# A two-layer decoder trunk in f32r: the moving operand of the large matmuls is walked in four sweeps, and the ring slots are shifted by 64 bytes

## The reference

```python
for i in range(2):                      # DEPTH
    if i == 0:
        h = h + stick_breaking_mixer(rmsnorm(h, sb_norm), w_qkv, w_o)    # 16 heads of 128
    else:
        h = h + chunked_gmlp_mixer(rmsnorm(h, gm_norm), w_in, v_norm, w_s, b_s, w_o)
    g, u = split(rmsnorm(h, ffn_norm[i]) @ w_gate_up[i], 2)              # 2048 x 11264
    h = h + (silu(g) * u) @ w_down[i]                                     # 5632 x 2048
return rmsnorm(h, final_norm)
```

## Time and profile before

| | |
|---|---|
| median of 2 runs | 2096.86 us (2096.85 to 2096.87) |
| the profiled execution | 2096.69 us |
| its span, first to last instruction | 2095.0 us |
| PE busy | 2085.6 us |
| DVE busy | 1430.4 us |
| ACT busy | 1012.8 us |
| DMA | 402.47 MB, mean 192 GB/s |
| granted TensorE clock, mean | 0.999 |

### The profile page before, as it was taken

The page is one execution under the profiler, slowest core; times in us unless marked ns, Lnnn a source line. Parts: engine busy times, 40 slices in busy tenths (PEclk is TensorE's granted clock), DMA queues, the critical chain, the costliest instruction groups (busy, mean ns, idle before and its releaser), DMA issues.

```text
span 2095.0 us, 27155 instructions
## 1 busy us (share of the span) xinstructions
PE 2085.6 (100%) x9279; PEld 1727.3 (82%) x9279; DVE 1430.4 (68%) x1822; ACT 1012.8 (48%) x1285; POOL 16.4 (1%) x30
## 2 busy tenths in 40 slices
PE   9999999999999999999999999999999999999998
PEld 7888888888888888888888888888888888888887
DVE  6787777867666666665557887877666676664444
ACT  6677765544444444444445444554444444444443
POOL 1000000000000000000000000000000000000000
PEclk9999999999999999999999999999999999999999
DMA  8564655666666666555567665566666666655554
GB/s 272 181 186 155 190 180 171 202 194 194 192 191 196 193 192 192 196 194 192 192 198 207 186 204 187 188 186 202 195 187 196 193 195 192 191 194 197 191 191 150
DMA packets 207419, 402.47 MB, mean 192 GB/s; under 512 B 12336, under 2 KB 13056, under 8 KB 206976
## 3 DMA queue, kind: packets, MB, share of 16 engines
q1 hardware_dynamic: 206496, 398.11, 60.9%
q0 software_dynamic: 688, 3.18, 0.4%
q10 hardware_dynamic: 176, 0.40, 0.1%
HBM read 399.55 MB, written 2.10 MB: 192 GB/s over the span
## 4 chain that ended last, share of the span: by engine, by line
PE 99%; issue 0%; ACT 0%; DVE 0%; POOLq 0%; POOL 0%; DVEq 0%; ACTq 0%
PE acc L1091 65%; PE acc L1097 32%; PE tp L1173 1%; PE tp L1193 0%; PE tp L1322 0%; PE acc L1139 0%; PE tp L1105 0%; PE acc L1132 0%; PE acc L1365 0%; PE acc L1364 0%; PE acc L1363 0%; ACT xT L372 0%; PE tp L1181 0%; PE tp L1125 0%; DVE h L1060 0%
## 5 line engine op out<-in xcount | busy, mean ns | idle before, releaser
L662 DVE TENSOR_TENSOR w_lo<-raw,w_hi 128x1024 fp32r<-128x1024 f32 x750 | 915.8, 1224 | 583.5 <-ACT w_hi L354 579.7
L354 ACT ACTIVATE w_hi<-raw 128x1024 fp32r<-128x1024 f32 x750 | 792.9, 1060 | 920.3 <-PE acc L1097 915.0
L1091 PE MATMUL acc<-w_hi,xT 128*128 128x512 f32 x4080 | 1010.3, 390 | 0.0
L1091 PEld LDWEIGHTS acc<-w_hi,xT 128*128 128x128 f32 x4080 | 764.7, 188 | 157.9
L1097 PE MATMUL acc<-w_lo,xT 128*128 128x512 f32 x2040 | 545.3, 389 | 0.0
L1097 PEld LDWEIGHTS acc<-w_lo,xT 128*128 128x128 f32 x2040 | 383.0, 188 | 79.6
L1091 PE MATMUL acc<-w_hi,hid_hi 128*128 128x512 f32 x944 | 368.4, 390 | 0.0
L1091 PE MATMUL acc<-w_hi,hid_lo 128*128 128x512 f32 x944 | 367.3, 389 | 0.0
L1097 PE MATMUL acc<-w_lo,hid_hi 128*128 128x512 f32 x944 | 252.3, 389 | 0.0
L1097 PEld LDWEIGHTS acc<-w_lo,hid_hi 128*128 128x128 f32 x944 | 177.2, 188 | 36.8
L1091 PEld LDWEIGHTS acc<-w_hi,hid_lo 128*128 128x128 f32 x944 | 177.3, 188 | 36.7
(11 more groups left out here) (117 smaller groups left out, 429.4 us busy)
## 6 DMA issues: line engine op xcount, KB each, us to landing
raw<-in_ffn_w_gate_up SPq DMA_DIRECT2D x352, 512.0 KB, 4.5
raw<-in_ffn_w_down SPq DMA_DIRECT2D x176, 512.0 KB, 3.6
raw<-in_sb_w_qkv SPq DMA_DIRECT2D x95, 512.0 KB, 4.4
raw<-in_gm_w_in SPq DMA_DIRECT2D x64, 512.0 KB, 4.2
raw<-in_sb_w_o SPq DMA_DIRECT2D x32, 512.0 KB, 4.1
raw<-in_gm_w_o SPq DMA_DIRECT2D x32, 512.0 KB, 3.9
h<-in_x SPq DMA_DIRECT2D x3, 512.0 KB, 8.9
gain_bc<-in_gm_v_norm POOLq DMA_DIRECT2D x1, 1024.0 KB, 6.8
```

Of the source, the lines that this page charges most:

```text
L354: nc.scalar.activation(w_hi[:, p % RING], raw[:, p % RING], ACT.Copy).then_inc(hi_ready, 1)
L662: nc.vector.tensor_tensor(w_lo[:, p % RING], raw[:, p % RING], w_hi[:, p % RING].bitcast(f32), ALU.subtract).then_inc(lo_ready, 1)
L1091: nc.tensor.matmul(acc_at(chunk, r), part[:, kt, rs], w_hi[:, p % RING, k], start=(kt == 0 and part is hi), stop=False)
```

## The change

The matmuls with weights as moving operand are told to take its 512 columns, and to write the 512 columns of acc, in another order. `swept` turns a row of 512 columns into a pattern of 4 sweeps x 32 runs x 4 columns: the first sweep takes columns 0-3, 16-19, 32-35 and so on, the second 4-7, 20-23 and so on. Four f32 columns are 16 bytes, and the runs of a sweep are 64 bytes apart. Operand and output are rearranged alike, so each column still goes to its own place. The stationary operand, the number of instructions, all waits and the tensors' contents are as before. The row is 128 x 512 in every case.

`ring` allocates w_hi and w_lo with 16 more columns per slot, so that a slot stands 4160 bytes behind the one before it: slots 0 to 3 at 0, 64, 128 and 192 bytes off a multiple of 256. A whole ring is then 16640 bytes, again a multiple of 256. W0 is the address at which w_hi began, and `region` is kept at a multiple of 512 bytes from it.

```diff
+    LINE, SWEEPS = 4, 4
...
-        w_hi = sb("w_hi", [P, RING, KP, CH], f32r)
-        w_lo = sb("w_lo", [P, RING, KP, CH], f32r)
+        STEP = 16
+
+        def ring(name):
+
+            return sb(name, [P, RING, KP * CH + STEP], f32r)[:, :, 0:KP * CH].rearrange("p s (k n) -> p s k n", k=KP)
+
+        w_hi = ring("w_hi")
+        w_lo = ring("w_lo")
+        W0 = nc.lookup_mloc(raw).addr + RING * KP * CH * 4
...
-        lead_in = sb("lead_in", [P, (nc.lookup_mloc(w_hi).addr - used_up_to) % CH // 4])
+        lead_in = sb("lead_in", [P, (W0 - used_up_to) % CH // 4])
...
+        def swept(columns):
+
+            return columns.rearrange("p (c h e) -> p h c e", h=SWEEPS, e=LINE)
...
-                            nc.tensor.matmul(acc_at(chunk, r), part[:, kt, rs], w_hi[:, p % RING, k],
+                            nc.tensor.matmul(swept(acc_at(chunk, r)), part[:, kt, rs], swept(w_hi[:, p % RING, k]),
                                              start=(kt == 0 and part is hi), stop=False)
...
-                        last = nc.tensor.matmul(acc_at(chunk, r), hi[:, kt, r * P:(r + 1) * P],
-                                                w_lo[:, p % RING, k], start=False, stop=(kt == K - 1))
+                        last = nc.tensor.matmul(swept(acc_at(chunk, r)), hi[:, kt, r * P:(r + 1) * P],
+                                                swept(w_lo[:, p % RING, k]), start=False, stop=(kt == K - 1))
```

More of the change, by code:

```diff
@@ L106, in hybrid_trunk @@
         used_up_to = nc.lookup_mloc(moments).addr + 32
-        lead_in = sb("lead_in", [P, (nc.lookup_mloc(w_hi).addr - used_up_to) % CH // 4])
+        lead_in = sb("lead_in", [P, (W0 - used_up_to) % CH // 4])
         region = sb("region", [P, 2 * KF * S])
         R0 = nc.lookup_mloc(region).addr
-        assert (R0 - nc.lookup_mloc(w_hi).addr) % CH == 0
+        assert (R0 - W0) % CH == 0
         HB = KF * S * 4
@@ L1138, in early_products @@
                 for r in range(RT):
-                    last = nc.tensor.matmul(acc_at(0, r), part[:, kt, r * P:(r + 1) * P], weight[:, p, k],
+                    last = nc.tensor.matmul(swept(acc_at(0, r)), part[:, kt, r * P:(r + 1) * P], swept(weight[:, p, k]),
                                             start=(kt == 0 and part is xT_hi and weight is w_hi), stop=False)
@@ L1356, in _ @@
                 rs = slice(r * P, (r + 1) * P)
-                dst = acc_at(1, r)
+                dst = swept(acc_at(1, r))
                 for t in range(ROWWISE, 2 * PF):
@@ L1362, in _ @@
                         kt = (t - PF) * KP + k
-                        nc.tensor.matmul(dst, hid_hi[:, kt, rs], w_hi[:, t % RING, k], start=False, stop=False)
-                        nc.tensor.matmul(dst, hid_hi[:, kt, rs], w_lo[:, t % RING, k], start=False, stop=False)
-                        last = nc.tensor.matmul(dst, hid_lo[:, kt, rs], w_hi[:, t % RING, k], start=False,
+                        nc.tensor.matmul(dst, hid_hi[:, kt, rs], swept(w_hi[:, t % RING, k]), start=False, stop=False)
+                        nc.tensor.matmul(dst, hid_hi[:, kt, rs], swept(w_lo[:, t % RING, k]), start=False, stop=False)
+                        last = nc.tensor.matmul(dst, hid_lo[:, kt, rs], swept(w_hi[:, t % RING, k]), start=False,
                                                 stop=(kt == KF - 1))
```

## The result

The changed kernel took 2113.4 us (median of 2 runs, 2113.0 to 2113.8) against 2096.9 us: slower by 0.8%, ratio 1.0079 with a 95% interval of 1.0062 to 1.0095. The forecast was 2010 us and faster. The range of 1995 to 2185 us holds the time, the direction is wrong. 16.6 us over 9024 matmuls are 1.8 ns for each: 228.5 ns where there were 226.7.

The account below looks back on a forecast made before the run. PE was taken as the bound, its 9024 large matmuls at 226.7 ns each. Sweeps saved 87 us, the slot shift counted 0: 2096.7 - 87 = 2010 us, range 1995 to 2185 us.

Parts of the forecast that it names:

- The reading of the bound: Large weight matmuls: PE busy throughout, 226.7 ns each, 13.3 ns over their columns; 9024 of them make 2045.5 us.
- other engines have no part in it: Large matmuls: the 13.3 ns extra does not come from other engines; 226.4 ns each where neither ACT nor DVE converts.
- the return to 1.81 and 0.91 us: Weight matmuls behind L1193: after 1.85 and 0.92 us, the usual times for eight and four matmuls come back.
- Step (1): Swept column order in all 9024 large matmuls: 217 ns each, saving 9.7 ns, 87 us in all.
- The floor of 215.8 ns: Lower bound of one swept matmul, 213.3 plus 2.5 ns: saves 10.9 ns each, 98 us, giving 1999 us.
- Step (2): w_hi and w_lo slots 4160 bytes apart: bounded at -7 to +13 ns per matmul, mean +4.6, taken as 0.
- The working cause: Large matmuls: PE's moving-weight reads and the next load's stationary reads clash, settling into a rhythm costing 32 cycles.
- no change: Rival for large matmuls: each 16-byte piece of weight load costs one cycle anywhere; 226.7 ns stay, 2097 us; chance 0.27.
- Other phases, worse rhythm: Rival: sweeps or four distances hold large matmuls at 231 ns, +41 us, 2138 us, or 236 ns, 2181 us; chance 0.11.
- The jump has a price: Rival: one cycle per 64-byte block left, 128 cycles per large matmul, 266.7 ns, +361 us, 2458 us; chance 0.15.
- a pattern by slot that repeats every four: Sign in large-matmul pieces: if the cause is right and distances matter, pieces of the four slots differ from each other.

Follow-up runs that it names:

- the kernel with neighbours above: TensorE stretches of 72 matmuls in the decoder's operand sequence, alone or beside ACT copies, DVE subtractions or both, decoder left out: 220.0 to 220.1 ns at 208 bytes.
- The best version found: Changed kernel's four sweeps kept, slots 4096 bytes apart again, both rings 208 bytes off: 2039.5 us, ratio 0.9726 to the kernel before.
- the sixteen distances: TensorE-only kernel, decoder left out, stretches of 36 plain-order matmuls at distances in steps of 16 bytes: 226.7 ns at 0 and 240, others 229 to 235.
- two experiments here: Changed kernel with evenly spaced slots, rings meant 208 and 48 bytes off, by the addresses at 224 and 64: 2095.7 and 2066.7 us.

## Why the prediction was wrong

The reading of the bound was right: the step between starts, 226.7 ns, with 13.3 ns over the columns, and PE alone on the path. That other engines have no part in it held for the plain order, and for four sweeps at 208 bytes; at 48 and 64 bytes it is open (the kernel with neighbours above). The rows broke off before the return to 1.81 and 0.91 us that I cited from them; the trace has it at 107.18 us. The best version found gains 57 us where I forecast 87 for the change.

Step (1) failed in its size: 87 us were forecast for the sweeps, and by themselves they gained 15. I took 217 ns for the swept order, from the rows of other operand types and an argument on why the clash should vanish. The argument was about an order, and the order has no value of its own: four sweeps take from 220 to 232 ns by the distance, and at distance 0 in the decoder 225 or 226.5 (2081 and 2095 us). Even the best is 6.7 ns over the columns, not 3.7. The floor of 215.8 ns was never reached; the lower end of the range, 1995 us, lies even below the 1999 us of that floor.

Step (2), the shift put at nothing, is the one that turned the sign. I wrote that no row tests another distance, bounded the shift by the phases seen after interruptions (-7 to +13 ns, mean +4.6) and then took 0. The kernel's regularity should have been read the other way: all 9024 matmuls stood at one distance, and I had no reason to call it an average one. By the sixteen distances it was among the two best for its order; three slots of four moved to 229, 232 and 233 ns. With the four values of the plain order the sum would have been (226.7 + 228.9 + 232.1 + 233.3) / 4 = 230.3 ns, +32 us for the shift alone; measured +39. The rest is in slots 0 and 1, which took 228.3 and 230.3 ns among neighbours at other distances and not 226.7 and 228.9: in the plain order the change of distance costs something too.

The working cause fell in part. The step depends on the distance between the two operands' addresses and not on either address; that fits two read streams of PE that influence each other, though no run shows the reads themselves. But that the weight load makes the extra by what it reads is refuted by the stretch with one stationary column. The Trainium skill states in "SBUF — State Buffer" that PE has a second, independent read port for weight loads. If that meant full independence in time, the distance would not matter; the measured 226.8 against 228.9 and 233.1 ns decide against that reading here.

The rivals: "no change" at 2097 us was closer than the forecast and is refuted in its mechanism, since 1 or 4 columns are no cheaper. "Other phases, worse rhythm" named the right mechanism for the shift. That its 2138 us meet the 2136 of the shift alone is luck: its 231 ns came from the pieces behind an interruption, not from another distance. "The jump has a price" is refuted: two sweeps at 128 bytes are 231 ns in an order that leaves each 64 bytes twice, where a cycle for each of these 64 jumps would make 240, and four sweeps go below the plain order. Longer jumps of the same 16-byte runs do cost: 241 to 249 ns with eight sweeps (128 bytes) and 276 to 279 with sixteen (256 bytes).

The warning on PSUM in the Trainium skill's "Advanced Engine Details and Errata", section PSUM Cachelines, does not hold in its first sentence for runs of four columns (the output swept alone: 8.19 against 8.16 us for 36 matmuls) and does not contradict its second, that two consecutive elements should stay together. The Trainium skill's 215.7 ns for a matmul of 512 columns ("TensorE: Matmul & The Clock Gate", section "Wait — 56ns, not 53.3ns?") agree with the 215.8 ns here for bf16 and are not reached in f32r.

What I said would show it was useful: a pattern by slot that repeats every four was named for the case that the distances matter, and it is the first thing that the chain after shows.

**Open.** What in TensorE or its reads makes the extra of f32r at one column per cycle, 6.7 to 21 ns per matmul at multiples of 16 bytes, when one stationary column does it as well as 128; every matmul here has a weight load before it. And why the changed kernel has 229.1, 228.0, 226.3 and 231.7 ns in its four slots, where the same four distances by twelve, in another sequence of operands, gave 226.6, 223.4, 229.5 and 226.8: with four sweeps and the distance changing, the values of the distances by themselves do not carry over.

## What to carry to other kernels

Take the step between starts of back-to-back matmuls, not their duration, and compare it with columns over clock; if it is above by a constant, and the operands are f32r as here, the distance of the moving from the stationary operand modulo 256 bytes is a parameter to be measured. A kernel that stands at one distance everywhere is at a point of that curve, and spreading it over several takes the average or, as here in the plain order, a little more (231 ns against 230.3). Measure the points alone, in one small kernel with a line per point, before touching the large one, and enter each point in more than one way, since a stepped order can have several rhythms. Then read the real addresses: an allocator that rounds made two experiments here test something else than their names say.

## What the hardware did that I had not expected

- f32r matmuls of 512 columns settle into repeating patterns of steps. The same stretch with four sweeps at 64 bytes has a rhythm of 220.0 ns and one of 223.3, and one program had executions at 2081 and at 2095 us on one chip.
- The extra depends on the distance to a few bytes: plain order, 226.7 ns at 0, 238.3 at 4, 233.3 at 8, 229.4 at 12 and 231.5 at 16 bytes.
- Fewer stationary columns do not lower it: 231, 231, 226.7, 231 and 232 ns with 1, 4, 8, 16 and 32 columns at distance 0 in the plain order, 226.7 with 128.
- Plain f32 at two cycles a column and bf16 at one keep 2.5 ns over their columns at every distance tried (0, 64 and 128 bytes).
